# Seven block products in place of eight for the MLP's up projections of a fused two-layer trunk

## The chip, the cores and the metric

The kernel runs on one core of a Trainium2 chip. The metric is the device time of one execution in microseconds (us). Before the change it is 1857.52 us, the median of 3 runs (1856.43 to 1858.48).

## The reference, cut to what matters

The model is a decoder trunk of two layers over 528 positions (16 meta tokens and 512 tokens) with 1024 channels, all in float32. Each layer is

```
u = rms_norm(h, norm_mix);  proj = u @ w_in                  # 1024 -> 7168
conv branch, differential attention, sigmoid gates -> merged
h = h + merged @ w_o                                         # 1024 x 1024
u = rms_norm(h, norm_mlp)
h = h + square(relu(u @ w_up)) @ w_down                      # 1024 -> 4096 -> 1024
return h[:, 16:528]
```

The change is in the MLP, the last two of these lines. In the second layer the 16 meta positions are no longer needed there, so its MLP runs over 512 positions and that of the first over 528.

## The kernel before, in words

Channels lie on the 128 partitions, in 8 chunks, and positions on the free axis. Every weight is cut into slabs of 1024 rows by 256 columns (128 partitions x 2048 elements, 1 MB). A layer has 68 slabs in a fixed order: 8 of the GLU, 12 of v, q and k, 8 of gates, 4 of w_pw, 4 of w_o, and 32 of the MLP.

A product in float32 is made of three in the PE's rounded format, float32r: with w = w_hi + w_lo and u = u_hi + u_lo it is w_hi u_hi + w_hi u_lo + w_lo u_hi. So each slab passes these steps. SP's queue loads it into one of two buffers `w_raw[:, b]` (L493), after `w_ready` says that the slab two before it has been split. The high part is a rounding copy into `w_hi[:, b]` and the low part is `w_raw - w_hi` into `w_lo[:, b]`, in 16 pieces of 128 columns. In `split` (L503 to L516) POOL makes both, after a one-element `tick`; in `split_low` (L518 to L523) POOL makes the low part and ACT the high one (`w_high_part`, L955 to L960). Both need the buffer's former slab to be used up (`w_used`). The MLP's slabs all go through `split`, those of w_pw and w_o through `split_low`. PE takes a slab in `a_slabs`: for each of its two column halves `a_tile` (L614 to L626) runs over 8 row blocks, 3 parts, and 2 halves of the positions (264 columns) in the first layer or all of them at once (512 columns) in the second. This is 96 matmuls of 264 columns, or 48 of 512, for a slab. The two column halves go to two slots of two PSUM banks, and `a_free` says that a slot has been read.

The MLP's order is `MLP_ORDER`: up 0, up 1, down 0, up 2, down 1, up 3, down 2, down 3, each of 4 slabs. For an up tile, ACT takes relu out of PSUM (L1152) and squares it, rounded, as the high part of `hid` (L1154); DVE squares relu again (L1562) and subtracts (L1563). For a down tile, DVE multiplies PSUM by the norm's reciprocal (L1591) and adds it to `h` (L1592). `hid` has two buffers, the second one `hid_b`. Ahead of the MLP, in the slabs of w_o, DVE adds each of the 8 tiles to `h` (L1549); ACT scales it, rounded, as `u2`'s high part and squares it for the norm's sum (`norm_tile`); DVE makes the low part (L1538) and the sum (L1541).

Every engine works its own list in program order, so an instruction that waits holds all that stand behind it. `announce` and `link` make an engine wait for its own instruction to be finished before the next.

Of the kernel before, what the change touches and what calls it, by code (L numbers as in the profile page):

```python
# [244 lines left out]
def build(nc, x_t, w_slabs, pvecs, rows_in, ident_in, mask_in, identb_in, out, h_spill, r_rows):  # L245
    ctx = ExitStack()
    with ctx:
# [254 lines left out]
        def _(pool):  # L502
# [110 lines left out]
        def _(pe):  # L613
            def a_tile(layer, slot, b, col, src, full=False, waits=None, blocks=range(NT)):  # L614
# [36 lines left out]
            def a_slabs(layer, slab, tile, n_turns, src, ready, full=False, hooks=(), middle=None, begin=None):  # L651
# [3 lines left out]
                def body(i, hooks=()):  # L655
                    hooks = list(hooks)
                    for b in range(1 if begin and isinstance(i, int) else 0, 2):
                        pe.wait_ge(w_ready, i * 2 + (s0 + b + 1))
                        for col in range(2):
# [1001 lines left out]
```

## Time and profile before

| | |
|---|---|
| median of 3 runs | 1857.52 us (1856.43 to 1858.48) |
| the profiled execution's own time | 1856.81 us |
| its span, first to last instruction | 1855.0 us |
| PE busy (matmuls) | 1831.2 us, 99% |
| POOL busy | 1333.3 us, 72% |
| DVE busy | 1119.0 us, 60% |
| ACT busy | 577.0 us, 31% |
| mean granted TensorE clock | 0.999 |
| bytes moved by DMA | 160.66 MB, mean 87 GB/s |

The span of the profiled execution is 1.8 us under its own time; what lies around it is the start and the end of the program. The profiled execution is 0.7 us under the median. PE's busy time is the union of its matmuls, whose ends are modelled, so the start of each of them, not its length, tells the pace. The MLP of the first layer runs from about 578 to 956 us of the span, that of the second from about 1491 us to the end.

### The profile page before, as it was taken

The numbers are of one execution on the slowest core, as the hardware profiler recorded it, in microseconds if no ns is written. First come the engines' busy times: TensorE is split into PE (matmuls) and PEld (weight loads), VectorE is DVE, ScalarE is ACT, GpSimd is POOL, SyncE is SP. The second block draws the span as 40 slices with busy tenths as digits, with TensorE's granted clock in tenths as the row PEclk, the third lists the DMA queues.
The fourth block names the chain that finished last, engine by engine and source line by source line (L and its number), as shares of the span: only waits on it lengthen the run. The fifth ranks groups of instructions, "written<-read, shape, count | busy, mean of one in ns | idle before, by whom it ended". The sixth has DMA issues, their size and how long they took to land.

```text
span 1855.0 us, 34632 instructions
## 1 busy us (share of the span) xinstructions
PE 1831.2 (99%) x12787; PEld 1652.2 (89%) x12787; DVE 1119.0 (60%) x1666; ACT 577.0 (31%) x1616; POOL 1333.3 (72%) x2400
## 2 busy tenths in 40 slices
PE   9999999999999999999999999999999999999999
PEld 9999888898999999999999998887768877888887
DVE  7998887877544333333468989888885433333233
ACT  4135565536332110101011246664362322010100
POOL 3767454646778888888898663436477799898985
PEclk9999999999999999999999999999999999999999
DMA  4221021112322222222232211111124222222222
GB/s 178 91 92 66 28 69 47 47 69 85 135 96 79 86 93 90 91 91 106 109 120 91 91 69 47 69 47 48 67 91 146 105 91 91 91 91 91 90 107 74
DMA packets 25550, 160.66 MB, mean 87 GB/s; under 512 B 3024, under 2 KB 3408, under 8 KB 7776
## 3 DMA queue, kind: packets, MB, share of 16 engines
q1 hardware_dynamic: 21888, 147.01, 22.4%
q10 hardware_dynamic: 3552, 12.15, 1.7%
q8 instruction: 73, 1.20, 0.3%
q14 instruction: 37, 0.30, 0.1%
HBM read 154.85 MB, written 4.29 MB: 86 GB/s over the span
## 4 chain that ended last, share of the span: by engine, by line
PE 87%; POOL 7%; DVE 2%; issue 2%; ACT 2%; POOLq 0%; DVEq 0%; ACTq 0%
PE psum L625 63%; PE psum L714 15%; POOL w_lo L515 4%; PE psum L744 2%; PE psum L776 2%; PE psum L764 1%; POOL w_lo L522 1%; POOL w_hi L513 1%; ACT e L978 1%; PE psum L752 1%; DVE mx L1259 1%; PE psum L646 1%; PE psum L821 1%; PE psum L793 1%; PE psum L632 0%
## 5 line engine op out<-in xcount | busy, mean ns | idle before, releaser
L625 PE MATMUL psum<-u,w_hi 128*128 128x264 f32 (+1 forms) x4416 | 900.5, 316 | 9.7 <-POOL w_lo L515 5.6
L515 POOL TENSOR_TENSOR w_lo<-w_raw,w_hi 128x128 fp32r<-128x128 f32 x1504 | 759.9, 543 | 7.8
L625 PEld LDWEIGHTS psum<-u,w_hi 128*128 128x128 f32 x4416 | 666.8, 189 | 68.1 <-issue 9.1
L625 PE MATMUL psum<-u,w_lo 128*128 128x264 f32 (+1 forms) x2208 | 558.8, 313 | 0.0
L522 POOL TENSOR_TENSOR w_lo<-w_raw,w_hi 128x128 fp32r<-128x128 f32 x640 | 314.3, 530 | 123.1 <-ACT w_hi L960 83.8
L625 PEld LDWEIGHTS psum<-u,w_lo 128*128 128x128 f32 x2208 | 362.5, 189 | 25.0
L714 PE MATMUL psum<-w_hi,u 128*128 128x256 f32 (+1 forms) x1856 | 337.1, 284 | 2.6 <-ACT v_sb L936 1.5
L467 DVE SCALAR_TENSOR_TENSOR psum<-xg,pvec,psum 128x512 f32<-128x512 f32 x440 | 300.9, 751 | 4.6 <-DVE xg L1399 2.2
L714 PEld LDWEIGHTS psum<-w_hi,u 128*128 128x128 f32 (+1 forms) x1856 | 264.8, 172 | 11.5 <-issue 3.1
L714 PE MATMUL psum<-w_lo,u 128*128 128x256 f32 (+1 forms) x928 | 259.7, 280 | 0.0
L1562 DVE TENSOR_TENSOR relu<-relu 128x528 f32<-128x528 f32 (+1 forms) x64 | 66.2, 1034 | 234.8 <-ACT u L1154 119.7
L1152 ACT ACTIVATE relu<-psum 128x528 f32<-128x528 f32 (+1 forms) x64 | 38.7, 605 | 459.9 <-PE psum L625 459.9
L513 POOL TENSOR_SCALAR w_hi<-w_raw 128x2048 fp32r<-128x2048 f32 x94 | 180.4, 1919 | 0.0
L512 POOL TENSOR_TENSOR tick<-ones 128x1 f32<-128x1 f32 x94 | 19.8, 211 | 218.8 <-PE psum L625 196.4
L625 PE MATMUL psum<-hid_b,w_hi 128*128 128x264 f32 (+1 forms) x768 | 163.9, 322 | 0.1
L714 PEld LDWEIGHTS psum<-w_lo,u 128*128 128x128 f32 (+1 forms) x928 | 159.7, 172 | 3.7
L1591 DVE TENSOR_TENSOR down_tmp<-psum,r_inv 128x512 f32<-128x512 f32 (+1 forms) x56 | 39.1, 699 | 190.3 <-PE psum L625 190.3
L567 POOL TENSOR_TENSOR rtmp<-raw,tabs 128x640 f32<-128x640 f32 x16 | 25.0, 1562 | 153.1 <-DVE q_scale L1221 101.9
L625 PEld LDWEIGHTS psum<-hid_b,w_hi 128*128 128x128 f32 x768 | 118.7, 188 | 12.0 <-issue 0.6
L625 PE MATMUL psum<-hid_b,w_lo 128*128 128x264 f32 (+1 forms) x384 | 102.4, 321 | 0.0
L978 ACT ACTIVATE e<-psum,nb,q_scale 128x272 f32<-128x272 f32 (+4 forms) x144 | 83.8, 585 | 35.8 <-DVE nb L1265 35.8
L960 ACT CAST w_hi<-w_raw 128x2048 fp32r<-128x2048 f32 x40 | 76.6, 1915 | 48.6 <-PE psum L625 48.6
(190 smaller groups left out, 1963.0 us busy)
## 6 DMA issues: line engine op xcount, KB each, us to landing
w_raw<-w_slabs SPq DMA_DIRECT2D x135, 1024.0 KB, 4.9
h<-x_t SPq DMA_DIRECT2D x4, 528.0 KB, 7.2
h<-x_t ACTq DMA_DIRECT2D x1, 2112.0 KB, 10.7
h_spill<-h ACTq DMA_DIRECT2D x8, 264.0 KB, 2.2
h<-h_spill ACTq DMA_DIRECT2D x1, 2112.0 KB, 10.4
out<-h SPq DMA_DIRECT2D x8, 256.0 KB, 2.0
r_b<-r_rows ACTq DMA_DIRECT2D x1, 1584.0 KB, 6.5
r_b<-r_rows ACTq DMA_DIRECT2D x1, 1536.0 KB, 7.4
```

The lines of the kernel that those rows point to most:

```text
L467: return nc.vector.scalar_tensor_tensor(out=done if ends else acc, in0=x, scalar=w, in1=done if begins else acc, op0=ALU.mult, op1=ALU.add)
L513: chain.link(nc.gpsimd.tensor_scalar(w_hi[:, b, :], w_raw[:, b, :], 1.0, 1.0, ALU.mult, ALU.mult))
L515: last = nc.gpsimd.tensor_tensor(w_lo[:, b, c:c + P], w_raw[:, b, c:c + P], w_hi[:, b, c:c + P], ALU.subtract)
L522: last = nc.gpsimd.tensor_tensor(w_lo[:, b, c:c + P], w_raw[:, b, c:c + P], w_hi[:, b, c:c + P], ALU.subtract)
L625: last = nc.tensor.matmul(psum[:, 2 * slot + j, 0:n], w[:, b, cut], src[:, part, kc, at0:at0 + n], start=(kc == 0 and m == 0), stop=(kc == ...
L714: last = nc.tensor.matmul(psum[0:tn, n % 2, 0:2 * P], u[:, part, kc, t0:t0 + tn], w[:, b, kc * 2 * P:(kc + 1) * 2 * P], start=(kc == 0 and ...
L744: nc.tensor.matmul(psum[0:tn, banks[c], at0:at0 + k1 - k0], qk[rows64, 0, hh % 2, qp, t0:t0 + tn], qk[rows64, 1, hh % 2, kp, k0:k1], start ...
L960: nc.scalar.copy(w_hi[:, b, :], w_raw[:, b, :]).then_inc(w_high, 1)
L978: ins = nc.scalar.activation(e[0:tn, c, E_OFF[i]:E_OFF[i] + w], psum[0:tn, banks[c], S_AT[i]:S_AT[i] + w], ACT.Exp, bias=nb[0:tn, c, i:i + ...
L1152: nc.scalar.activation(row(relu[:, j, :], layer), a_ps(layer, j), ACT.Relu).then_inc(a_free[j], 1)
L1562: link(V.tensor_tensor(relu2[:, lo:lo + n], relu[:, j, lo:lo + n], relu[:, j, lo:lo + n], ALU.mult))
L1591: announce(dve, V.tensor_tensor(row(down_tmp[:], layer), a_ps(layer, j), row(r_inv2[:], layer), ALU.mult), a_free[j], a_read(layer, A_MLP ...
```

## The change: what it does

The up projections alone are computed by the scheme of Strassen in Winograd's form. A slab's 1024 rows and 256 columns are cut in two each way into quarters A11, A21, A12, A22 of 512 rows by 128 columns (the host lays them out so, `quads`), and the activations into quarters of 512 channels by half of the positions. From sums of weight quarters (S1 to S4) and of activation quarters (T1 to T4) seven products are made, where there were eight. Each is 4 row blocks x 3 parts = 12 matmuls of 264 columns (first layer) or 256 (second), 84 for a slab. They stand in the order p1, p5, p2, p6, p7, p4, p3, and `P_BANK` gives their PSUM banks; p1 and p6 share bank 6, p5 has bank 7, p7 bank 3.

The MLP's order becomes up 0, down 0, up 1, down 1, and so on. The down slabs take `split_low` on POOL and the high part from ACT (`down_high`). `hid` has one buffer. An up slab's four first forms (A11, S1, A12, S2) get their low part in another way: ACT writes the rounded negative into `w_lo` (`early_neg`), and two DMAs that POOL issues add `w_raw` and `s2` to it in place (`early_low`). The three other forms (A22, S3, S4) keep POOL's subtraction, 4 pieces of 128 columns each (`late_parts`). DVE makes the sums of weights and of products. The diff is condensed below: several statements stand on one line, and waits are named after `#`.

```
+A_TILES = A_MLP + 32
+MLP_ORDER = [(what, g) for g in range(4) for what in ("up", "down")]
+PRODUCTS = [(F_A11, G_B11, "p1"), (F_S1, G_T1, "p5"), (F_A12, G_B21, "p2"), (F_S2, G_T2, "p6"), (F_S3, G_T3, "p7"), (F_A22, G_T4, "p4"), (F_S4, G_B22, "p3")]
+P_BANK = {"p1": (6, 6), "p6": (6, 6), "p5": (7, 7), "p2": (0, 4), "p3": (1, 5), "p4": (2, 2), "p7": (3, 3)}
 SP, the load of the slab two ahead of up slab m:
+    sp.wait_ge(low_landed[n % 2], 32 * (n // 2 + 1)); sp.wait_ge(w_form, n + 1); sp.wait_ge(late_low, 2 * n + 1); sp.wait_ge(sum_late, n + 1)
 POOL:
+def early_low(g, m):
+    pool.wait_ge(w_neg, n + 1)
+    chain.link(nc.gpsimd.tensor_tensor(tick[:], ones[:, 0:1], ones[:, 0:1], ALU.mult))
+    pool.dma_start(w_lo[:, b, 0:3 * QUAD], w_raw[:, b, 0:3 * QUAD], accum_op=ALU.add).then_inc(low_landed[b], 16)
+    pool.dma_start(w_lo[:, b, 3 * QUAD:SLAB], s2[:, b, :], accum_op=ALU.add).then_inc(low_landed[b], 16)
+def late_parts(g, m, parts):      # per part: wait w_late, 4 x tensor_tensor 128x128 into x_lo
+order: early_low(g,1) | late_parts(g,1,plain) early_low(g,2) late_parts(g,1,summed) late_parts(g,2,plain) early_low(g,3)
+       late_parts(g,2,summed) late_parts(g,3,all) | 4 x down_low | early_low(g+1,0) late_parts(g+1,0,all)
 PE:
+def up_products(layer, g, m):
+    pe.wait_ge(low_landed[b], ...); pe.wait_ge(w_form, n + 1); pe.wait_ge(c22_done, n)
+    # p6: p1_done; p2: a_free of both slots (m < 2) or hid_ready 2(n-1); p7: hid_ready 2n-1, late_low 2n+2; p3: w_ready s+1
+    for kc in range(KH):
+        for j, (w, act_) in enumerate([(hi, uh), (hi, ul), (low, uh)]):
+            last = nc.tensor.matmul(quad(layer, m, name), w[:, cut], act_[:, x, kc, 0:n2], ...)
 ACT, in the slabs of w_o, tile i:
+    if i == NT - 3: early_neg(layer, 0, 0)
+    if i == NT - 1: early_neg(layer, 0, 1)
+    norm_raw(layer, i); form_plain(layer, i)
+    if i == NT - 1: late_plain(layer, 0, 0)
+    form_sum(layer, i)
+    if i == NT - 1: first_product(layer, 0, 0); late_sums(layer, 0, 0)
+    if i >= KH: form_last(layer, i)
+    norm_square(layer, i)
+    if i == NT - 2: early_high(layer, 0, 0)
+    if i == NT - 1: early_high(layer, 0, 1)
 ACT, up slab m:
+    if m == 3: down_high(layer, g, 0)
+    if m == 0 and g: early_neg(layer, g, 1)
+    if m or g: first_product(layer, g, m)
+    if m == 1 and g == 0: late_sums(layer, g, 1)
+    if m: hidden_high(layer, g, m - 1, 0)              # relu, then its square
+    if m == 1 and g == 0: early_neg(layer, g, 2)
+    if m < 3: late_plain(layer, g, m + 1)
+    if m < 3 and (m or g): early_high(layer, g, m + 1)
+    if m == 1 or m == 0 and g: early_neg(layer, g, m + 2)
+    if m < 3 and (m or g): late_sums(layer, g, m + 1)
+    hidden_high(layer, g, m, 1)
+def early_neg: wait sum_early; wait w_used s-1 (m < 2) or q_full of p6 two slabs before; 2 x nc.scalar.mul(..., -1.0), 1536 and 512 columns
+def early_high: 2 x nc.scalar.copy, 1536 and 512 columns;  late_plain: copy of 512;  late_sums: wait sum_late; copy of 1024
 DVE, in the slabs of w_o, tile ch: add to h;  if ch == 7: sums_late(0, 0);  form_norm(ch);  if ch in (4, 5): sums_early(0, ch - 4)
 DVE, up slab m:
+    if m: c12_sum(g, m - 1); (g, m) == (0, 1): read the norm's sum; hidden_low(g, m - 1, 1); square_up(g, m - 1, 0)
+    if m == 1 and g == 0: sums_early(g, 2)
+    if m < 3 and (m or g): sums_late(g, m + 1)
+    if m: hidden_low(g, m - 1, 0)
+    if m == 1 or m == 0 and g: sums_early(g, m + 2)
+    u2_sum(g, m); c22_sum(g, m); c21_sum(g, m); square_up(g, m, 1)
+    if m == 0 and g == 0: sums_late(g, 1)
+def sums_early: 2 dependent tensor_tensor of 512 columns in w_raw and s2;  sums_late: wait w_ready of the slab before; 2 of 512
+def u2_sum: wait p6; U2 = p6 + P1, T = p5 + U2;  c22_sum: p2 += P1; wait p7; U3 = p7 + U2; p7 = p5 + U3 -> c22_done
+def c21_sum: wait p4; p4 += U3 -> tile_sum;  c12_sum: wait p3; p3 += T -> tile_sum
+def square_up: wait relu; in place in PSUM max(x, 0) * relu;  hidden_low: wait its square; subtract -> hid_ready
+form_norm(ch), ch < 4: wait u_raw; T1; 2 subtractions; the sum of squares.  ch >= 4: T2, T4, T3 (264), 3 subtractions (528, 264, 528), the sum
 DVE, down slab d of g < 3: if d == 3: sums_late(g + 1, 0);  after its first tile, d > 1: sums_early(g + 1, d - 2)
```

## Rows read from the trace of the kernel before

**Rows 1.** The page, part 1 (PE's line) and part 2 (the granted clock by slice).
```profile
PE 1831.2 (99%) x12787; PEld 1652.2 (89%) x12787; DVE 1119.0 (60%) x1666; ACT 577.0 (31%) x1616; POOL 1333.3 (72%) x2400
...
PEclk9999999999999999999999999999999999999999
```
**Rows 2.** The page, part 4: the chain that ended last, by engine and line.
```profile
PE 87%; POOL 7%; DVE 2%; issue 2%; ACT 2%; POOLq 0%; DVEq 0%; ACTq 0%
PE psum L625 63%; PE psum L714 15%; POOL w_lo L515 4%; PE psum L744 2%; PE psum L776 2%; PE psum L764 1%; POOL w_lo L522 1%; POOL w_hi L513 1%; ACT e L978 1%; PE psum L752 1%; DVE mx L1259 1%; PE psum L646 1%; PE psum L821 1%; PE psum L793 1%; PE psum L632 0%
```
**Rows 3.** Windows: stretch, length, busy of PE, PEld, DVE, ACT, POOL; clock, DMA.
```profile
588.00:681.50 93.50, 93.36 (x764) 93.02 (x763) 32.71 (x34) 18.88 (x30) 84.24 (x145) 1.00 0.26 90
1491.50:1580.40 88.90, 88.28 (x378) 70.38 (x377) 34.77 (x37) 19.82 (x32) 84.09 (x140) 1.00 0.27 95
```
**Rows 4.** Timeline of PE, first layer, up slab: start, length, instruction, count.
```profile
870.47 0.65 PE L625 MATMUL psum<-u,w_hi 128*128 128x264 f32 x4
...
879.23 0.65 PE L625 MATMUL psum<-u,w_hi 128*128 128x264 f32 x4
```
**Rows 5.** Timeline of PE, second layer.
```profile
1599.96 0.62 PE L625 MATMUL psum<-u,w_hi 128*128 128x512 f32 x2
...
1603.43 0.64 PE L625 MATMUL psum<-u,w_hi 128*128 128x512 f32 x2
```
**Rows 6.** Timeline of PE, products of 256 columns for q, k and v.
```profile
249.92 0.40 PE L714 MATMUL psum<-w_hi,u 128*128 128x256 f32 x2
...
253.46 0.40 PE L714 MATMUL psum<-w_hi,u 128*128 128x256 f32 x2
```
**Rows 7.** Groups by line and form, ACT: count, busy us, mean ns, idle before.
```profile
L960 ACT CAST w_hi<-w_raw 128x2048 fp32r<-128x2048 f32 x40 | 76.6, 1915 | 48.6 <-PE psum L625 48.6
L945 ACT COPY raw<-psum 128x256 f32<-128x256 f32 x64 | 23.6, 368 | 47.0 <-PE psum L714 46.7
L1152 ACT ACTIVATE relu<-psum 128x528 f32<-128x528 f32 x32 | 19.6, 612 | 235.5 <-PE psum L625 235.5
L1154 ACT ACTIVATE hid_b<-relu 128x528 f32 x16 | 10.4, 648 | 2.1
```
**Rows 8.** The same groups on DVE.
```profile
L1592 DVE TENSOR_TENSOR h<-h,down_tmp 128x528 f32 x24 | 32.6, 1360 | 3.8 <-DVE down_tmp L1591 3.8
L1562 DVE TENSOR_TENSOR relu<-relu 128x528 f32<-128x528 f32 x32 | 34.3, 1072 | 120.4 <-ACT u L1154 61.4 <-ACT hid_b L1154 59.0
L1591 DVE TENSOR_TENSOR down_tmp<-psum,r_inv 128x512 f32<-128x512 f32 x32 | 22.1, 692 | 106.4 <-PE psum L625 106.4
L1591 DVE TENSOR_TENSOR down_tmp<-psum,r_inv 128x528 f32<-128x528 f32 x24 | 17.0, 708 | 83.9 <-PE psum L625 83.9
L467 DVE SCALAR_TENSOR_TENSOR psum<-xg,pvec,psum 128x512 f32<-128x512 f32 x440 | 300.9, 751 | 4.6 <-DVE xg L1399 2.2 <-DVE o_ms L1293 0.2
```
**Rows 9.** Timeline of DVE: an instruction that waits for the one before it.
```profile
634.54 0.71 DVE L1563 TENSOR_TENSOR hid_b<-relu,hid_b 128x528 f32 x1 [0.18 <-DVE relu L1562]
```
**Rows 10.** Timeline of POOL: an MLP slab's split, and a low part alone (w_o).
```profile
545.04 7.89 POOL L522 TENSOR_TENSOR w_lo<-w_raw,w_hi 128x128 fp32r<-128x128 f32 x16 [4.45 <-ACT w_hi L960]
...
613.61 0.19 POOL L512 TENSOR_TENSOR tick<-ones 128x1 f32<-128x1 f32 x1 [1.00 <-PE psum L625]
613.76 1.91 POOL L513 TENSOR_SCALAR w_hi<-w_raw 128x2048 fp32r<-128x2048 f32 x1
615.76 8.49 POOL L515 TENSOR_TENSOR w_lo<-w_raw,w_hi 128x128 fp32r<-128x128 f32 x16
```
**Rows 11.** Timeline of DVE: the last tiles of w_o are added to h.
```profile
560.64 0.71 DVE L1549 TENSOR_TENSOR h<-psum,h 128x528 f32<-128x528 f32 x1 [3.59 <-PE psum L625]
...
578.16 0.71 DVE L1549 TENSOR_TENSOR h<-psum,h 128x528 f32<-128x528 f32 x1 [3.44 <-PE psum L625]
```
**Rows 12.** The page, parts 3 and 6: the slabs' queue and one load.
```profile
q1 hardware_dynamic: 21888, 147.01, 22.4%
...
w_raw<-w_slabs SPq DMA_DIRECT2D x135, 1024.0 KB, 4.9
```

More of the change, by code:

```diff
@@ new lines, in late_parts @@
+                def late_parts(g, m, parts):
+                    b, n = m % 2, up_nth(layer, g, m)
+                    for k in parts:
+                        source = w_raw[:, b, 3 * QUAD:SLAB] if k == 0 else s34[:, (k - 1) * QUAD:k * QUAD]
+                        if k < 2:
+                            pool.wait_ge(w_late, 2 * n + k + 1)
+                        for c in range(0, QUAD, P):
+                            cut = slice(k * QUAD + c, k * QUAD + c + P)
+                            last = nc.gpsimd.tensor_tensor(x_lo[:, b, cut], source[:, c:c + P], x_hi[:, b, cut], ALU.subtract)
+                        last.then_inc(late_low if k < 2 else w_ready, 1)
@@ L649, in first_slab, with a_slabs @@
                             last.then_inc(w_used if col else a_full, 1)
-            def a_slabs(layer, slab, tile, n_turns, src, ready, full=False, hooks=(), middle=None, begin=None):
+            def a_slabs(layer, slab, tile, n_turns, src, ready, full=False, hooks=(), middle=None, begin=None, pairs=False):
                 s0, n0 = layer * SLABS + slab, layer * A_TILES + tile
@@ L669, in body @@
                             else:
-                                last = a_tile(layer, 2 if third else col, b, col, src, full, ready if not (b or col) else None)
+                                last = a_tile(layer, 2 if third else col, b, col, src, full, ready if not (b or col) else None, pairs=pairs)
                             last.then_inc(w_used if col else a_full, 1)
@@ L682, in partition_sums, with mlp_sums @@
+            def mlp_sums(layer):
+                source, sums = mlp_sum(layer)
+                pe.wait_ge(n_summed, layer + 1)
+                for j in range(2):
+                    last = nc.tensor.matmul(sums[:, j, :], ones[:], source[:, j, :], start=True, stop=True)
+                last.then_inc(st_full, 1)
             def partition_sums(layer, ready, value, src, full=False, cols=False):
@@ L1168, in _ @@
                             act.dma_start(h_spill[:, ch, :], h[:, ch, :]).then_inc(spilled, 16)
+                    else:
+                        down_high(layer, g, 2)
+                        down_high(layer, g, 3)
+                        if g < 3:
+                            early_neg(layer, g + 1, 0)
+                            late_plain(layer, g + 1, 0)
+                            late_sums(layer, g + 1, 0)
+                            early_high(layer, g + 1, 0)
         @block.vector
@@ L1596, in down_body @@
                                     link(ins)
-                        turns(dve, NT // 2, down_body, chain, 0 if g == 3 else 2)
+                                if j == 0 and d > 1 and g < 3:
+                                    sums_early(g + 1, d - 2)
 def kernel(**inputs):
```

441 lines of the change are left out of this document (370 added, 71 removed).

## The prediction

> **What bounds the kernel now.** Read the page's busy shares first, then the chain, then the windows of the MLP. PE is busy 99% of the span at a granted clock of nine tenths or more in every slice, the upper of its two levels, 2.4 GHz [rows 1]. The chain that ended last is 87% PE, and 63% is the one matmul line L625; POOL follows with 7%, nearly all of it splits [rows 2]. In the windows of two up stages (eight slabs) PE has no gap worth naming: 93.36 of 93.50 us, 88.28 of 88.90 us [rows 3]. So a matmul less is time won, as long as no other engine becomes late. In the same windows POOL is busy 84 us, 90% and 95%, while DVE has 33 to 35 us and ACT 19 to 20: one engine has almost no room and two have much [rows 3].
>
> **What is removed.** The pace is read from starts. First layer: from 870.47 to 879.23 are 12 periods of 6 matmuls, 0.1217 us each for 264 columns [rows 4]. Second: 15 matmuls of 512 columns in 3.47 us, 0.231 each [rows 5]. 256 columns with a weight load each, as the new products have, stand at 30 matmuls in 3.54 us, 0.118 each [rows 6]; so the extra weight loads of the second layer are in that pace already. An up slab goes from 96 x 0.1217 = 11.68 to 84 x 0.1217 = 10.22 us, and from 48 x 0.231 = 11.1 to 84 x 0.118 = 9.9. With 16 up slabs a layer that is 23.4 + 19.1 = **42.5 us** at most. It is kept only where everything else fits into 10.2 or 9.9 us a slab.
>
> **Prices.** ACT: 2048 columns 1.915, 528 take 0.648, so 0.834 ns a column: 1536 and 512 together 2.12, 1024 1.06, 512 0.63; relu 0.61; the copy of a product 0.37 [rows 7]. DVE: 692 and 708 ns for 512 and 528 columns give 1 ns a column, 264 columns 0.44; relu's square in place as L467, 0.77 [rows 8]; each instruction that waits for its forerunner adds 0.18 [rows 9]. POOL: 0.49 a piece (7.89 / 16) [rows 10]. Where both DVE operands lie in SBUF and POOL is at work, 264 to 528 columns wait: L1562 takes 1.07 against 0.71 for the same form right behind it, L1592 1.36 [rows 8, 9]. I take 0.36 more where POOL works, and 0 where it waits; the ends are 0 and 0.65. A pair `sums_early` is then 1.74, `sums_late` 1.38, plus that.
>
> **The new DMAs.** No row shows a DMA that adds, or one issued by POOL. One from HBM to SBUF of the same 1 MB lands after 4.9 us [rows 12]; the slabs' queue has 22.4% of 1855 us for 147 MB, 2.96 us for 1 MB, so 1.9 us of the 4.9 are fixed. The lower end is 4.9. With two issues at 0.3 each (between POOL's tick of 0.19 and something above it [rows 10]) it is 5.5, which I take, as the nearest row moves the same bytes. If the bytes pass three times, 3 x 2.96 + 1.9 + 0.6 = 11.4 is the upper end. The Trainium skill speaks against my value: Collectives: The Full Stack, section The bandwidth ceiling, says that an adding transfer reads two sources and so runs at half the rate of a copy. By rows its data part would be 5.9 and the landing 8.4 us; that is the first rival. The page DMA: Bandwidth & Descriptors, section Latency and other measured facts, has about 1 us to the first byte for a DMA from GpSimd against 0.6 from SP; that would make my 5.5 about 5.9, and the sum 0.8 us longer.
>
> **The start of each MLP.** Let T be the end of w_o's matmuls (578.1), with tiles 4 to 7 full at T-17.5, -11.7, -5.8, 0 [rows 11]. For a tile above 3, DVE adds (0.71), waits for ACT's scaling (0.71 with hops), makes T2, T4, T3 (0.44 each, two waits), three subtractions (0.71, 0.44, 0.71) and the sum (0.89): 5.85, all of a tile's 5.84. `sums_early` comes on top at tiles 4 and 5. So tile 4 is left at T-9.6. Then ACT makes `early_neg` (2.12) ahead of its scaling of tile 5, and DVE leaves tile 5 at T-0.7. ACT's square of tile 6 ends at T+3.3 and `early_high(0, 0)`, behind it, at T+5.5: the first product starts there, not at T. On ACT follow `early_neg` 7.6, scaling of tile 7 8.3, plain forms 8.9 and 9.5, T2's form 9.95, the product's copy 10.3, `late_sums` 11.4; POOL's four pieces of S3 end at 13.4. p7 waits for these, and p7, p4 and p3 take 4.4 us: slab 0 ends at T+17.8 instead of 10.2 or 9.9. **Loss 7.6 + 7.9 = 15.5 us.** Ends: 11 (no ACT delay, no port waits) and 19 (port waits at 0.65).
>
> **Slab 1 of the first group** starts at T+17.8. DVE: square_up 18.9, sums_late 20.3, c12 20.9, the norm's sum 21.7, hidden_low 22.4; ACT's late_sums and relu end at 21.9, square_up 23.4, sums_early(2) with a port wait 25.4. ACT's early_neg(2) ends at 27.5, the DMAs land at 33.0. DVE's own list (sums_late after POOL's parts 27.9, hidden_low, sums_early, five sums of products) brings `c22_done` at 33.1, the same. Slab 2 should have started at 28.4. **Loss 4.7 + 5.0 = 9.7**; it grows by 2 us for each us that the landing grows.
>
> **Slab 1 of the six later groups.** From its start: p1 full 1.65, copy 2.05, relu 2.65, square_up 3.65, slab 1's low parts ready 3.7, sums_late 5.3, hidden_low 6.0, sums_early 7.7, then U2, T, P2 + P1, U3, p7's sum (3 x 0.62 + 2 x 0.44) 10.45. The next p1 waits for it: 0.2 over 10.22, 0.55 over 9.9. **Loss 2.3.** Its own start needs the landing of `early_neg(1)`, which can't begin before the down slab is used up: negative ready at +2.4, due at 10.2 or 9.9, so 7.8 or 7.5 us are there, and at 5.5 nothing is lost.
>
> **From up to down.** The first down slab takes the buffer of up slab 2. After that one is used up: ACT 1.92, POOL 16 x 0.49 = 7.9, hops, 10.0 us against slab 3's 10.22 or 9.9. But `down_high` stands behind relu and square of slab 2's tile, whose chain (c21_sum 20.6 after slab 1's start + 10.4 + 10.2) ends 1.3 or 1.6 late: loss 0.9 and 1.55, in the two first groups 0.2 and 0.5, where slab 2 started late. 3 x 0.9 + 3 x 1.55 + 0.7 = **8.1**. Before, POOL had 1.0 us of idle time here [rows 10]: the room is spent.
>
> **Down slabs.** POOL's 7.9 and ACT's 1.9 stand in 11.68 or 11.1 us; DVE's sums for the next group hold POOL twice. 1.5 us in all, ends 0 and 5. SP's loads come 5 us or more ahead of their use in every place above. The move of the order, relu2's loss and `hid` in one buffer cost nothing: down's row blocks 6 and 7 are needed 4.4 us after its start and are ready 1.1 us before; if that cover goes, it costs the same us.
>
> **Sum.** 15.5 + 9.7 + 2.3 + 8.1 + 1.5 = 37.1 lost of 42.5, 5.4 gained. The profiled execution took 1856.8 (span 1855.0 and 1.8 around it): 1851.4, and with 0.7 to the median **1852 us**.
>
> **Rivals.** (1) Slower: the bytes of the adding DMAs pass twice or more, since source and destination are both read, and they land late. At 8.4 us: 2 x 2.9 more at the first groups, 3 x 0.6 + 3 x 0.9 more at slab 1 of the others, 10.3: 1862. At 11.4 it is 2 x 5.9, 3 x 3.6 + 3 x 3.9, and slab 0, which has 9.3 us, loses 2.1 in six groups: 47, 1899. It turns slower than before by more than 3.7 us at about 8.4. For it: no row shows such a DMA at the copy's pace; against it: the engines are 22% used [rows 12]. (2) The chain on DVE is the bound: port waits of 0.65, as L1592 shows [rows 8], on each pair in slab 1 and at the starts give 6 x 0.6 + 3 = 6.6 more, 1858, no change. Against it: POOL waits much of the time. (3) The starts are cheaper, 11 and 6, and the turns to down cost nothing where ACT slips in earlier: 42.5 - 25 = 17 gained, 1841. For it: each of my chains takes the latest of several arrivals. That the products don't save their matmuls is excluded by rows 4 to 6.
>
> **Chances.** Forecast 38%, within 1846 to 1858; rival 1 30%; rival 2 17%; rival 3 15%. A measurement tells 0.2% (3.7 us) from no change. Faster: all of rival 3 and 27 of the forecast's 38, 42%; same 22%; slower 36%. The range, 1838 to 1885, takes in rival 3 and most of rival 1.
>
> **What would show it.** Right: an up slab's PE stretch of 10.2 and 9.9 us in slabs 2 and 3; the first product 5 us or more after w_o's last matmul, released by ACT w_hi; slab 2 of a first group released by the DMA; idle PE of 1 to 2 us ahead of each down stage, released by POOL w_lo. Wrong: a landing of the adding DMAs over 8 us, PE gaps ahead of slab 1 in later groups, or DVE busy under 8 us in a slab. A time under 1841 or over 1885 would say that a term is missing.

## The result and the profile after

The changed kernel takes 1882.51 us (1880.9 to 1883.81, 4 runs) where the kernel before takes 1856.97 on the same chip (1855.56 to 1858.48, 4 runs): ratio 1.0134, 95% interval 1.0122 to 1.0146. It is 25.5 us slower; 5 us faster was forecast. All readings below are of the profiled execution, span 1881.4 us, 26.4 longer than that of before.

The page first: PE's line, the granted clock by slice, and part 4 of the changed kernel.
```profile
PE 1809.6 (96%) x13173; PEld 1660.0 (88%) x13173; DVE 1296.5 (69%) x2074; ACT 832.9 (44%) x1912; POOL 1160.3 (62%) x2240
...
PEclk9999999999999999999999999999999989999999
...
PE 73%; POOL 7%; DVE 6%; DMA 6%; issue 4%; ACT 3%; DVEq 0%; POOLq 0%; ACTq 0%
PE psum L757 41%; PE psum L896 15%; PE psum L849 9%; DMA w_raw<-w_slabs 3%; DMA w_lo<-s 3%; POOL w_lo L597 3%; PE psum L926 2%; PE psum L958 2%; POOL w_lo L604 2%; PE psum L946 1%; POOL x_lo L715 1%; ACT e L1252 1%; PE psum L934 1%; DVE h L1991 1%; PE psum L778 1%
```
PE's share of the chain fell from 87% [rows 2] to 73%, and two transfers stand in it that were not there: the slab loads and the DMAs that add, 3% each. In busy time PE saved 21.6 us (1831.2 less 1809.6), but the span shows the waits. The same windows as in [rows 3], same columns (PE, PEld, DVE, ACT, POOL, granted clock, DMA share, GB/s). They hold other slabs now: the second begins in the last tiles of w_o, whose matmuls end at 1501.0 us here.
```profile
588.00:681.50 93.50, 85.82 (x687) 85.14 (x686) 53.24 (x78) 38.27 (x47) 62.60 (x132) 0.96 0.48 131
...
1491.50:1580.40 88.90, 77.95 (x475) 70.79 (x474) 55.36 (x91) 45.56 (x62) 52.25 (x108) 0.92 0.49 129
```
PE has 7.7 and 11.0 us of gaps (4.7 of the 11.0 are the wait for the first product of the second MLP) where it had almost none, and the clock is below the 1.00 of before.

**Where the time went.** An undisturbed up slab takes 10.19 us (84 matmuls, 0.1214 each) in the first layer and 9.97 (0.1187) in the second. Sixteen slabs each save 16 x 1.49 + 16 x 1.13 = 41.9 us (42.5 forecast). With the 26.4 us that the span grew, 68.3 us were lost again. Slab by slab, from PE's starts, in us (what a slab takes above 10.19 or 9.97, its wait at the end among it):

| place | forecast | measured |
|---|---|---|
| start of each MLP, to the start of slab 1 | 7.6 + 7.9 | 8.4 + 9.0 |
| first groups, slab 1 | 4.7 + 5.0 | 6.6 + 5.9 |
| first groups, slab 2 | 0 | 1.6 + 2.8 |
| six later groups, slab 0 | 0 | 6.4 |
| six later groups, slab 1 | 2.3 | 17.7 |
| six later groups, slab 2 | 0 | 9.2 |
| slab 3 and the turn to down | 8.1 | 0.8 |
| down slabs | 1.5 | about 3 |
| sum | 37.1 | 71.4 |

(The sum is 3.1 above 68.3: it charges every wait against an even pace, and the kernel before isn't at that pace throughout either. Its first MLP, 578.2 to 953.4 us, takes 1.4 us more than 32 x 11.68. In the other direction, 1.2 us of the 26.4 lie between the two MLPs, and part of them may be a stretch of 3.4 us at half clock at 1398 us, which the kernel before doesn't have there.) Of the 34 us that the forecast lacks, 31 stand in one kind of place, slabs 0 to 2 of the later groups: 33.3 us for 2.3.

**One such wait.** Group 1, first layer; slab 1 runs from 692.93. Timelines of POOL, SP's queue, DVE, ACT and PE (start, length, instruction, and in brackets the idle time before it and what ended it):
```profile
690.57 0.19 POOL L702 TENSOR_TENSOR tick<-ones 128x1 f32<-128x1 f32 x1 [1.26 <-ACT w_lo L1158]
691.06 0.89 POOL L703 DMA_DIRECT2D w_lo<-w_raw  x1 [0.30 <-POOL tick L702]
691.64 1.20 POOL L704 DMA_DIRECT2D w_lo<-s  x1
...
692.90 9.53 SPq L574 DMA_DIRECT2D w_raw<-w_slabs  x2
...
697.88 0.70 DVE L1928 TENSOR_TENSOR hid<-psum,hid 128x528 fp32r<-128x528 f32 x1
702.75 0.69 DVE L1850 TENSOR_TENSOR w_raw<-w_raw 128x512 f32<-128x512 f32 x1 [4.17 <-DMA w_raw<-w_slabs]
703.48 0.69 DVE L1851 TENSOR_TENSOR s<-w_raw 128x512 f32<-128x512 f32 x1
704.21 0.43 DVE L1898 TENSOR_TENSOR r_inv<-psum,r_inv 128x264 f32<-128x264 f32 x1
...
705.82 0.44 DVE L1907 TENSOR_TENSOR psum<-psum,q_u 128x264 f32<-128x264 f32 x1
...
704.21 1.48 ACT L1157 ACTIVATE w_lo<-w_raw 128x1536 fp32r<-128x1536 f32 x1 [5.51 <-DVE s L1851]
...
706.41 0.56 PE L849 MATMUL psum<-uh,w_hi 128*128 128x264 f32 x1 [2.99 <-DVE psum L1907]
```
SP's row holds two issues, the second at 702.10, so its length is not a landing. The load of slab 3 can't be issued before slab 1's low parts have landed, since the adding DMA reads `w_raw` too: 692.90. At that moment slab 2's adding DMAs are 1 to 2 us old. They share the 16 engines, and the load lands at 702.73, after 9.8 us for the usual 4.9. DVE has stood since 698.6 at the sums of slab 3, with the sums of C22 queued behind; PE, ready at 703.4, starts slab 2 at 706.4. All six later groups go this way: the load is issued at the start of slab 1 and takes 7.7 to 10.4 us, and DVE stands idle for 2.1 to 4.3 us. With the usual 4.9 us it would have landed at 697.8 (an estimate from these rows), before DVE asks for it. So it is the meeting of the two queues, on top of the late issue, that makes it late. The DMA view of 688 to 706 us shows the sharing (packets, MB, share of 16 engines; then KB and us to landing):
```profile
q0 software_dynamic: 544, 1.90, 59.9%
q1 hardware_dynamic: 262, 2.02, 30.3%
...
w_raw<-w_slabs SPq DMA_DIRECT2D x2, 1024.0 KB, 7.5
w_lo<-w_raw POOLq DMA_DIRECT2D x1, 768.0 KB, 6.6
w_lo<-s POOLq DMA_DIRECT2D x1, 256.0 KB, 10.4
```
The same bytes hold the engines twice as long when they are added: 18 x 0.599 / 1.90 = 5.7 us for 1 MB against 2.7. Over the whole execution, the page:
```profile
q1 hardware_dynamic: 21888, 147.01, 22.7%
q0 software_dynamic: 9216, 33.56, 9.7%
...
w_raw<-w_slabs SPq DMA_DIRECT2D x135, 1024.0 KB, 4.9
w_lo<-w_raw POOLq DMA_DIRECT2D x32, 768.0 KB, 6.0
w_lo<-s POOLq DMA_DIRECT2D x32, 256.0 KB, 7.0
```
0.097 x 1881.4 / 33.56 = 5.44 us per MB against 2.90 for the slabs. The Trainium skill, Collectives: The Full Stack, section The bandwidth ceiling, says of the reduce transfers of a ring that each add needs two source reads and so halves the rate of a copy. The trace agrees (1.9 times), though these transfers stay inside one SBUF.

**The clock.** Windows of the changed kernel, columns as above; the last is undisturbed work:
```profile
582.40:586.00 3.60, 3.51 (x17) 3.54 (x18) 2.30 (x5) 3.57 (x5) 1.32 (x3) 0.54 0.02 5
609.70:616.60 6.90, 3.07 (x14) 3.07 (x15) 2.65 (x5) 2.40 (x5) 5.29 (x11) 0.52 1.02 194
705.20:712.30 7.10, 5.89 (x27) 5.92 (x28) 4.35 (x9) 5.94 (x10) 5.71 (x13) 0.53 0.75 178
716.00:719.00 3.00, 3.00 (x27) 3.00 (x26) 1.80 (x5) 0.33 (x1) 3.00 (x8) 1.00 0.78 320
```
After PE's waits at 578, 607 and 703.4 us the granted clock is 0.5, the lower level (1.2 GHz), and the first matmuls of the next slab start 0.21 to 0.22 us apart for 0.12. There are eight such stretches with some 155 matmuls: about 14.8 us, counted in the table's first, third and sixth lines. Some 4 us of them cost nothing: the 42 slow matmuls in slab 0 of the two first groups stand ahead of p7, which waits for POOL afterwards all the same (1.5 us in the first layer, 0.7 in the second). The prediction had no such term.

### The profile page after: what moved, and what is told of

Read it like the earlier page. It is cut to its first block, busy times and chain, and to the rows that moved or that the text cites. A ratio compares the mean times of both kernels' runs of the same rounds, so it can differ in the third digit from the quotient of the medians.

```text
span 1881.4 us, 35177 instructions
## 1 busy us (share of the span) xinstructions
PE 1809.6 (96%) x13173; PEld 1660.0 (88%) x13173; DVE 1296.5 (69%) x2074; ACT 832.9 (44%) x1912; POOL 1160.3 (62%) x2240
## 3 DMA queue, kind: packets, MB, share of 16 engines
q0 software_dynamic: 9216, 33.56, 9.7%
## 4 chain that ended last, share of the span: by engine, by line
PE 73%; POOL 7%; DVE 6%; DMA 6%; issue 4%; ACT 3%; DVEq 0%; POOLq 0%; ACTq 0%
PE psum L757 41%; PE psum L896 15%; PE psum L849 9%; DMA w_raw<-w_slabs 3%; DMA w_lo<-s 3%; POOL w_lo L597 3%; PE psum L926 2%; PE psum L958 2%; POOL w_lo L604 2%; PE psum L946 1%; POOL x_lo L715 1%; ACT e L1252 1%; PE psum L934 1%; DVE h L1991 1%; PE psum L778 1%
## 5 line engine op out<-in xcount | busy, mean ns | idle before, releaser
L604 POOL TENSOR_TENSOR w_lo<-w_raw,w_hi 128x128 fp32r<-128x128 f32 x1152 | 548.9, 515 | 234.5 <-ACT w_hi L1234 195.2
L757 PE MATMUL psum<-u,w_hi 128*128 128x264 f32 (+1 forms) x2112 | 408.0, 308 | 8.9 <-POOL w_lo L597 5.0
L757 PEld LDWEIGHTS psum<-u,w_hi 128*128 128x128 f32 x2112 | 310.1, 189 | 31.1 <-POOL w_lo L597 6.5
L757 PE MATMUL psum<-hid,w_hi 128*128 128x264 f32 (+1 forms) x1536 | 328.4, 322 | 1.8 <-POOL w_lo L604 1.6
L757 PEld LDWEIGHTS psum<-hid,w_hi 128*128 128x128 f32 x1536 | 237.1, 188 | 26.6 <-issue 2.3
L757 PE MATMUL psum<-u,w_lo 128*128 128x264 f32 (+1 forms) x1056 | 251.1, 304 | 0.0
L597 POOL TENSOR_TENSOR w_lo<-w_raw,w_hi 128x128 fp32r<-128x128 f32 x480 | 237.4, 532 | 2.5
L757 PE MATMUL psum<-hid,w_lo 128*128 128x264 f32 (+1 forms) x768 | 204.8, 321 | 0.0
L849 PE MATMUL psum<-uh,w_hi 128*128 128x264 f32 (+1 forms) x512 | 154.2, 301 | 43.1 <-DVE psum L1907 17.2
L757 PEld LDWEIGHTS psum<-u,w_lo 128*128 128x128 f32 x1056 | 170.6, 189 | 8.5
L849 PE MATMUL psum<-ul,w_hi 128*128 128x264 f32 (+1 forms) x512 | 151.7, 296 | 0.0
```

Of the source, the lines that this page charges most:

```text
L597: last = nc.gpsimd.tensor_tensor(w_lo[:, b, c:c + P], w_raw[:, b, c:c + P], w_hi[:, b, c:c + P], ALU.subtract)
L604: last = nc.gpsimd.tensor_tensor(w_lo[:, b, c:c + P], w_raw[:, b, c:c + P], w_hi[:, b, c:c + P], ALU.subtract)
L757: last = nc.tensor.matmul(psum[:, 2 * slot + j, 0:n], w[:, b, cut], src[:, part, kc, at0:at0 + n], start=(kc == 0 and m == 0), stop=(kc == ...
L849: last = nc.tensor.matmul(quad(layer, m, name), w[:, cut], act_[:, x, kc, 0:n2], start=(kc == 0 and j == 0), stop=(kc == KH - 1 and j == 2))
```

## The experiments

Each run was timed in three rounds beside the kernel before, whose median on each chip was 1857.0 to 1857.7. Ratios are to it. "After" is the changed kernel, timed apart from these runs; the last column is the difference of the medians.

| run | us | ratio | 95% interval | us against after |
|---|---|---|---|---|
| e1_copy | 1841.08 | 0.9912 | 0.9896 to 0.9929 | -41 |
| e2_behind | 1896.04 | 1.0211 | 1.0194 to 1.0228 | +14 |
| e3_warm | 1877.22 | 1.0102 | 1.0086 to 1.0119 | -5 |
| e4_order | 1858.54 | 1.0003 | 0.9993 to 1.0012 | |
| e5_start | 1890.3 | 1.0182 | 1.0165 to 1.0199 | +8 |
| e6_half | 1846.41 | 0.9946 | 0.9929 to 0.9962 | -36 |
| e7_both | 1858.36 | 1.0009 | 0.9999 to 1.0020 | -24 |
| e8_behind_high | 1888.92 | 1.0172 | 1.0155 to 1.0189 | +6 |
| e9_split | 1841.65 | 0.9920 | 0.9903 to 0.9936 | -41 |
| e10_best | 1841.46 | 0.9917 | 0.9900 to 0.9934 | -41 |
| e11_first | 1876.18 | 1.0099 | 1.0082 to 1.0116 | -6 |
| e12_after_c21 | 1842.49 | 0.9925 | 0.9898 to 0.9953 | -40 |

**Copies for additions (e1_copy).**
```diff
-  pool.dma_start(w_lo[...], w_raw[...], accum_op=ALU.add)
+  pool.dma_start(w_lo[...], w_raw[...])        # and the same for s2
```


> The changed kernel with its 64 adding DMAs made plain copies of the same bytes (the low parts of the four early forms are then wrong). Theory A, the adding DMAs hold the 16 engines twice as long as a copy and push back the load of slab 3, whose sum blocks DVE's list: the software queue's share falls from 9.7% to about 5%, the landing from 7 to about 5 us, the load of slab 3 from 8 to 10 us back to 5, the PE gap ahead of slab 2 in the six later groups from 2.9 us each to under 1, and the first groups' gap by 2 to 3 us each; in all 15 to 22 us less, clock included, 1860 to 1867 us. Theory B, DVE's own chain with waits for the port it shares with POOL sets the gap: 0 to 4 us less, the gaps stay.

The copy leaves out the addition, so the four low parts hold the raw weights and sums. Every wait and byte count stays. 41 us went with the addition, where 15 to 22 were expected. Its queue and landings (the page), and group 1 of the first layer as windows, first of this kernel, then of the changed one:
```profile
q0 software_dynamic: 9216, 33.56, 5.1%
...
w_lo<-w_raw POOLq DMA_DIRECT2D x32, 768.0 KB, 4.0
w_lo<-s POOLq DMA_DIRECT2D x32, 256.0 KB, 4.6
```
```profile
669.20:704.50 35.30, 35.30 (x293) 35.30 (x293) 26.46 (x40) 23.09 (x31) 22.03 (x48) 1.00 0.61 201
```
```profile
669.20:704.50 35.30, 34.04 (x278) 33.62 (x277) 21.26 (x30) 18.59 (x24) 19.47 (x38) 1.00 0.78 188
```
0.051 x 1839.1 / 33.56 = 2.8 us per MB: a copy from SBUF to SBUF has the slabs' pace. The two windows are the same stretch of time, not the same work: group 1 begins at 676.0 us here and at 682.4 in the changed kernel. All 24 slabs of the later groups then take 10.19 or 9.97 us without a gap, and the turn to down costs nothing although slab 2 is on time. So what the adding DMAs cost in the later groups is the addition and not that there are DMAs at all. Most of it lies in the transfer: the landing of the first falls by 2.0 us, of which POOL's issue has 0.3 (0.57 us for 0.89).

**Sums of slab m+2 behind the sums of C22 (e2_behind).**
```diff
-  if m == 1 or m == 0 and g: sums_early(g, m + 2)
   u2_sum(g, m)
   c22_sum(g, m)
+  if m == 1 or m == 0 and g: sums_early(g, m + 2)
```


> The changed kernel with DVE's sums_early of slab m+2 behind c22_sum of slab m, where it stood ahead of u2_sum. Theory A (DVE's list is held by a late load, and c22_done behind it holds PE): the gap ahead of slab 2 in the later groups falls from 2.9 us to under 1, the stall partly coming back as a wait of p7 for POOL's late parts of slab 2; 5 to 12 us less in all. Theory B (the length of the chain of sums, not the wait for the load): sums_early's 1.5 us leave the chain, so at most 1.5 us each in six groups, and the gap ahead of slab 2 in the first groups, which waits for the landing, stays.

If DVE's order were the cause, the gap ahead of slab 2 would go. It went from 17.7 to 12.4 us in the six later groups, and a new one of 2.5 us came ahead of slab 3 in each; both theories expected a faster kernel, and it is 14 us slower. Slab 2's own adding DMAs now go out 0.5 to 2.1 us after the start of slab 1, for 1.4 to 3.1 us ahead of it, and land at 10.3 to 12.1. PE's first matmuls of slabs 2 and 3, group 1:
```profile
704.60 0.36 PE L849 MATMUL psum<-uh,w_hi 128*128 128x264 f32 x1 [1.99 <-DVE psum L1907]
...
719.05 0.36 PE L849 MATMUL psum<-uh,w_hi 128*128 128x264 f32 x1 [2.29 <-DVE psum L1907]
```
The sums, the negative and the adding DMA of slab 3 are one loop with the loads; what is put back in one place comes due in the next.

**Dummy matmuls in PE's waits (e3_warm).**
```diff
+  if (g, m) == (0, 0): 18 matmuls of ones into an unused bank
+  if m == 2: 24 of them (8 in later groups), ahead of the wait for slab 2
   pe.wait_ge(low_landed[b], 32 * (n // 2 + 1))
```


> The changed kernel with matmuls of ones by ones in PE's waits: 18 ahead of the first up slab of a layer, 24 ahead of slab 2 of the first group, 8 ahead of slab 2 of the later groups. Theory C, PE's idle time there is followed by a stretch at the lower granted clock that costs 14.8 us beside the gaps themselves: the granted clock stays at 1.0 through the MLP, and 8 to 14 us less. Rival: the slow stretches come from something else (the DMA traffic, POOL), and the clock falls all the same: no change, or slower by what the added matmuls overrun.

The clock's mean rose from 0.988 to 0.996, and of eight slow stretches in the MLPs two were left, one in slab 0 of each layer. Only 5.3 us were won: in group 1, slab 1's start to slab 3's start is 23.5 us for 26.4, but slab 0 of the first group took 15.1 for 13.6 us, with a wait of 2.5 us at p7. There p7 starts 13.4 us after w_o's last matmul in both kernels, since POOL's low parts set it; the faster first products only made the wait ahead of it longer, and the half clock came behind it (18 matmuls, 17 in the second layer). The same place as above, 705 us, in windows of this kernel and of the changed one:
```profile
700.00:723.00 23.00, 22.22 (x182) 21.88 (x182) 15.26 (x27) 13.56 (x18) 13.54 (x30) 1.00 0.57 162
```
```profile
703.00:719.30 16.30, 13.31 (x88) 13.13 (x87) 11.91 (x21) 9.70 (x13) 10.36 (x23) 0.79 0.72 195
```
So the clock's share is real, but it is won back only where no later wait of the same slab takes it. In one of the six later groups the dummies also ran past the wait, and slab 2 started 0.65 us later, counted from slab 1's start, than without them.

**The order alone (e4_order).** The kernel before, with up and down groups alternating.
```diff
-MLP_ORDER = [("up", 0), ("up", 1), ("down", 0), ("up", 2), ...]
+MLP_ORDER = [(what, g) for g in range(4) for what in ("up", "down")]
```


> The kernel before with the MLP's order alone changed to up 0, down 0, up 1, down 1. All theories: within 1 us of the kernel before, since the hidden chunks 6 and 7 are ready 1 us or more ahead of use. A rival: each of the 8 turns from up to down waits 0.5 us or more, 4 us slower.

No change: this part of the edit is free, as forecast.

**Half of the adding DMAs' bytes (e6_half).**
```diff
-  scalar.mul(w_lo[0:3Q], w_raw[0:3Q], -1.0); scalar.mul(w_lo[3Q:4Q], s2, -1.0)
+  scalar.mul(w_lo[0:2Q], w_raw[0:2Q], -1.0)
-  pool.dma_start(w_lo[0:3Q], w_raw[0:3Q], accum_op=add); pool.dma_start(w_lo[3Q:4Q], s2, accum_op=add)
+  pool.dma_start(w_lo[0:2Q], w_raw[0:2Q], accum_op=add)
+  # VectorE, after w_form: w_lo[2Q:3Q] = w_raw[2Q:3Q] - w_hi[2Q:3Q]; w_lo[3Q:4Q] = s2 - w_hi[3Q:4Q]
```


> The changed kernel with half of the adding DMAs' bytes: ScalarE's negatives and the adding DMA cover the block A11 and the sum S1 alone (512 KB in one DMA for 1 MB in two), and the low parts of A12 and S2 are made by VectorE as raw minus high, two 512-column subtractions a slab, placed where VectorE is idle. Theory A (the loop slab load, sums, negative, adding DMA, next load is what binds the later groups, and the second pass of the adding DMA's bytes is what makes it too long): landing falls from 6-7 us to 3.5-4.5 us, the gaps ahead of slab 2 in later groups (1.2 to 4.0 us) go, granted clock is full there, total 1840 to 1850, near the 1841 that plain copies gave. Rival (a fixed cost of an adding DMA, its issue and latency, not its bytes): landing stays over 5.5 us and the total at 1870 to 1880. Second rival (VectorE, 8.7 of 10.2 us busy in slab 1, now gets 1.4 us more): PE waits for the sums of C22 or for the hidden tiles in slabs 1 and 2, 1855 to 1875.

The edit has one more part, which the cut leaves out: in the last down slab ACT copies the high parts of the next slab 0 ahead of its late parts. What that part is worth alone was not run; e7, e9, e10 and e12 have it too.

1846.4: 36 us below after, 11 below before. The landing is 4.6 us. The gaps ahead of slabs 1 and 2 are gone in the later groups and the clock there is full. There the load of slab 3 goes out 2.9 to 3.5 us ahead of slab 1's start, where it went out at that start before, and lands 2.4 to 3.7 us into it. The first product of each MLP also comes 0.9 us earlier, which fits the shorter negatives ahead of its high copy on ACT. One wait is new, at p2 of slab 2, 1.1 to 1.3 us in the six later groups. DVE, POOL and PE around it:
```profile
695.84 0.44 DVE L1921 TENSOR_TENSOR psum<-psum,q_u 128x264 f32<-128x264 f32 x1
696.32 3.89 DVE L1859 TENSOR_TENSOR w_lo<-w_raw,w_hi 128x512 fp32r<-128x512 f32 x1
700.13 0.68 DVE L1860 TENSOR_TENSOR w_lo<-s,w_hi 128x512 fp32r<-128x512 f32 x1
...
696.00 3.65 POOL L716 TENSOR_TENSOR x_lo<-s,x_hi 128x128 fp32r<-128x128 f32 x8
...
700.86 0.39 PE L852 MATMUL psum<-uh,w_hi 128*128 128x264 f32 x1 [0.93 <-DVE w_lo L1860]
```
Two equal subtractions took 3.89 and 0.68 us. The first begins 0.3 us behind the start of eight POOL subtractions in a row and ends 0.6 us after them.

**Away from POOL's run (e9_split).** Its low part of A12 for slab 2 moved ahead of `u2_sum` of slab 1, where POOL stands; the one of S2 stays.
```diff
+  if m == 1: low_form(g, 2, A12)
   u2_sum(g, m); c22_sum(g, m); c21_sum(g, m)
-  if m in (1, 2): low_form(g, m + 1, A12 and S2)
+  if m in (1, 2): low_form(g, m + 1, S2 if m == 1 else A12 and S2)
```


> The kernel with half of the adding DMAs' bytes, and VectorE's low part of A12 for slab 2 moved from behind the C21 sum to ahead of the U2 sum of slab 1 (the low part of S2 stays behind). In its parent that 512-column subtraction took 3.9 us for its usual 0.69 because it began beside a back-to-back run of eight GpSimd subtractions, and PE's p2 of slab 2 waited 1.2 to 1.4 us in all eight groups. Theory (the place beside the GpSimd run is what costs): the wait at p2 goes, total 1846.4 less 8 x 1.3 = 1836, 1834 to 1840. Rival (VectorE's slack of 1 us in slab 1 is used up, so the sums of C22 come late by as much): 1842 to 1848.

The wait at p2 of slab 2 is gone in every group, and 4.8 us of the hoped 10 came, a time between the theory's and the rival's: waits of 0.35 us came ahead of slab 3 in the second layer and of 0.36 to 0.56 at the end of slab 3 in both, and the first groups, to the end of slab 3, stayed within 0.4 us. POOL's run still holds DVE, now at the subtraction that stayed (slab 1 of group 1, second layer):
```profile
1597.50 3.33 DVE L1863 TENSOR_TENSOR w_lo<-s,w_hi 128x512 fp32r<-128x512 f32 x1
```
It took 3.1 to 3.3 us in all eight groups. Moving it away from POOL's run as well was not tried.

**The first group as the others (e10_best, e11_first).** Sums, negative and adding DMA of slab 2 go out during slab 0; e10 on top of e9, e11 on top of after.
```diff
   c21_sum(g, m)
+  if m == 0 and g == 0: sums_early(g, 2)          # DVE; was ahead of sums_late at m == 1
+  if m == 1 and g == 0: early_neg(layer, g, 2)    # ACT; was behind hidden_high
   first_product(layer, g, m)
-  late_parts(g, 1, plain + summed); early_low(g, 2)
+  late_parts(g, 1, plain); early_low(g, 2); late_parts(g, 1, summed)   # POOL
```


> As the kernel before it in this list, and the first group treated as the later ones: sums, negative and adding DMA of slab 2 are issued during slab 0 and the turn to slab 1, ahead of the first product's copy and the summed low parts of slab 1. Theory (the 3.4 us gap ahead of slab 2 of the first group and the slow clock after it come from where slab 2's early chain stands in the written order): gap under 1 us, no half clock in slab 2, 4 to 5 us less in each layer, 1826 to 1832. Rival (the wait moves to p7 of slab 1, whose low parts are made later, or to the gap ahead of slab 1): 1834 to 1840.

> The changed kernel with that treatment of the first group alone (the adding DMAs carry all their 1 MB). If the gap of 6.5 and 5.8 us ahead of slab 2 in the first group is made by the written order, it falls to the 2 to 4 us of the later groups, with less half-clock time: 1882.5 less 2 x (3 to 5) = 1872 to 1877. If it is made by the adding DMA's landing, 1879 to 1884.

e10: 1841.46, no change from e9, where its theory had 1826 to 1832 and its rival 1834 to 1840. e11: 6.3 us below after, as its first theory said; the gap ahead of slab 2 fell there from 6.5 and 5.8 to 4.0 and 4.1. What is left of it in e10 has another releaser, the load of slab 3:
```profile
604.25 0.69 DVE L1854 TENSOR_TENSOR w_raw<-w_raw 128x512 f32<-128x512 f32 x1 [0.35 <-DMA w_raw<-w_slabs]
...
608.50 0.43 PE L854 MATMUL psum<-uh,w_hi 128*128 128x264 f32 x1 [2.92 <-DVE psum L1920]
```

**Slab 3's sums behind C21, first group only (e12_after_c21).**
```diff
-  if m == 1 or m == 0 and g: sums_early(g, m + 2)     # ahead of u2_sum
+  if g and m < 2: sums_early(g, m + 2)
   u2_sum; c22_sum; c21_sum
+  if m == 1 and g == 0: sums_early(g, 3)
```


> The best kernel so far (half of the adding DMAs' bytes, the split low part, the first group's slab 2 early) with VectorE's sums of slab 3 in the first group alone moved behind the C21 sum of slab 1. There the load of slab 3 lands 9.7 us into slab 1, and the sums of C22 stood behind it in VectorE's order. Theory (in the first group, unlike in the later ones, it is the order on VectorE that makes the gap ahead of slab 2): the gap of 3.2 and 3.0 us falls under 0.5 us, slab 2 runs at full clock, nothing new ahead of slab 3, 1841.5 less 6 to 9 = 1832 to 1836. Rival (the loop through the adding DMA binds here too, as it did in the later groups when the sums were moved behind): the gap comes back ahead of slab 3, 1839 to 1843.

The rival held. PE's first matmul of slab 2, its p6, and the first of slab 3:
```profile
606.64 0.36 PE L854 MATMUL psum<-uh,w_hi 128*128 128x264 f32 x1 [1.10 <-DVE psum L1920]
...
612.05 0.36 PE L854 MATMUL psum<-uh,w_hi 128*128 128x264 f32 x1 [0.79 <-ACT r_inv L1189]
...
619.87 0.36 PE L854 MATMUL psum<-uh,w_hi 128*128 128x264 f32 x1 [1.75 <-DVE psum L1920]
```
One gap of 3.2 us became three (start to start 1.4, 1.1, 2.0 with the matmul's own 0.12 in each), and slab 3 starts at 619.9 where it started at 620.3.

**The start (e5_start, e7_both).**
```diff
   norm_raw(layer, i)
-  if i == NT - 1: early_neg(layer, 0, 1)                # stood ahead of norm_raw
+  if i == NT - 2: early_high(layer, 0, 0)               # now ahead of norm_raw
   norm_square(layer, i)
+  if i == NT - 1: early_neg(layer, 0, 1); early_high(layer, 0, 1)
```


> The changed kernel with ScalarE's order at the start of an MLP alone changed: the high parts of up slab 0 are copied two output tiles earlier (ahead of the raw norm copy of channel 6), and the negatives of slab 1 stand behind the last channel's forms, just ahead of slab 1's high parts. Theory (what holds the first product is the 2.0 us high copy queued behind the forms of channel 6, and what holds the first slab's p2 and p7 is the last channel's forms queued behind slab 1's negatives): first product at T+2.0 to T+3.0 instead of T+4.45 and T+5.08, slab 0 ends 2 us earlier in each layer, total 1877 to 1880. If slab 1's adding DMAs, now issued some 6 us later, become the bound at once: slab 1 starts no earlier and the time is 1881 to 1887. Rival (the start is set by VectorE's forms of the last channel): first product earlier, but p2 waits longer by the same amount, 1881 to 1884.

> The two edits above together (half of the adding DMAs' bytes; high parts of slab 0 earlier at the start of an MLP). Theory A: the gains add up, since the later groups' loop and the start are different places: 1836 to 1846. Rival: with the loop relaxed the start gains nothing more, time as with half of the bytes alone.

Both missed: 1890.3 for e5 where no theory went above 1887, and 1858.4 for e7 where 1836 to 1846 was expected. In e5 the first product came at once, 0.5 us after the last w_o matmul for 4.45, and slab 0 took 22.3 us for 13.6:
```profile
578.65 0.39 PE L849 MATMUL psum<-uh,w_hi 128*128 128x264 f32 x1 [0.24 <-DMA w_lo<-s]
...
594.63 0.59 PE L849 MATMUL psum<-uh,x_hi 128*128 128x264 f32 x1 [5.22 <-POOL x_lo L715]
```
POOL issues slab 1's adding DMAs ahead of slab 0's late low parts; with the negatives moved back, it waits for them and p7 waits for POOL. My theory had moved an instruction on ACT and not asked who stands behind its reader on POOL.

**The first product's copy behind the high parts (e8_behind_high).**
```diff
-  first_product(layer, g, m)
   hidden_high(layer, g, m - 1, 0); late_plain(...); early_high(layer, g, m + 1)
+  first_product(layer, g, m)
```


> The changed kernel with one part of the edit undone: ScalarE's copy of the first product stands behind the high parts of the coming slab (still ahead of the negatives of the slab after it). Theory: PE's p6 waits for that copy, which then ends 5.3 to 6.0 us into a slab for 4.4 us needed, so each of 24 to 32 up slabs loses 0.9 to 1.6 us: 1905 to 1925. Rival (PE waits later in the slab for the adding DMAs' loop anyway, so that the earlier wait is free where the gap ahead of slab 2 shrinks by as much): 1882 to 1895.

6 us slower than after: the rival's answer. p6 waits 0.75 to 2.3 us in most slabs, slab 1's among them (in the two first groups it waits 6 us there, and the gap ahead of slab 2 is gone):
```profile
698.95 0.39 PE L849 MATMUL psum<-uh,w_hi 128*128 128x264 f32 x1 [0.72 <-ACT r_inv L1185]
```
but the gap at the slab's end falls by a part of it (2.96 us for 3.27 in group 1). So this part of the edit is worth 6 us as the kernel stands; what it is worth where the loop doesn't bind was not run.

## Why the prediction was wrong

- **The pace.** Right: 10.19 and 9.97 us for 10.22 and 9.9, 41.9 us for 42.5.
- **The start.** Right in size (17.4 us for 15.5) and in mechanism: the first product is released by the high copy that stands behind the forms of tile 6, at T+4.4 (5.5 forecast), and p7 by POOL at T+13.4 in the first layer, as worked out. Of the difference 0.7 us in each layer is the norm's sum, four matmuls that PE runs between slabs 0 and 1 and that the sum didn't count.
- **Slab 1 of the first groups.** Right in mechanism, 12.4 us for 9.7: slab 2 is released by the adding DMA, whose landing took 7.9 us in the first layer for the 5.5 of the sum.
- **Slabs 0 to 2 of the later groups: the step that failed.** It was the sentence that SP's loads come 5 us or more ahead of their use in every place. The load of slab 3 is issued when slab 1's low parts have landed and is wanted some 6 us into slab 1; it landed 7.7 to 10.4 us in. I followed each landing to PE, and not to the next load that waits for it, and I counted each transfer as if it were alone. The places cost 33.3 us for 2.3; 6.4 of these are slab 0's wait for slab 1's landing, which I had put at nothing. e1, e2 and e6 show it from three sides: the addition taken away (33 us of these places gone), DVE's order changed (the gap only moves), half of the bytes (the gaps at the slabs' ends gone). Two of the prediction's signs of being wrong are there as well: gaps ahead of slab 1 in all six later groups (0.3 to 1.8 us), and landings over 8 us.
- **The DMAs that add.** The landing was mis-sized: from the first issue to the last landing 7.1 to 8.0 us alone and over 11 beside a load (691.06 to 702.09), for 5.5. Rival 1 named the cause and had the sign, but with 1862 at a landing of 8.4 us it was 20 us short, as it shared the missing step and counted no meeting of the two queues.
- **From up to down: 8.1 forecast, 0.8 found.** e1 has slab 2 on time and no wait at the turn either, so a late slab 2 is not what covers it; the chain of latest arrivals on ACT was too pessimistic, as rival 3 said.
- **The clock.** 14.8 us by count, some 4 of them hidden ahead of p7, missing from the sum. It is not a separate cause: each stretch follows a wait. e3 gave back 5.3 of it.
- **DVE's port waits** (what the prediction calls the extra time of a DVE instruction while POOL works) were charged at 0.36 a pair. Mostly they are 0 to 0.3, but a few in the up slabs of the changed kernel are 1.0 to 1.9 us and some in its down slabs up to 3.1, and in e6 there are some of 3.2, where an instruction begins beside a long POOL run. Rival 2, which had them as the bound, is out: in e1 DVE is busy for 8.70 us of slab 1's 10.20 in group 1, in the changed kernel for 7.93 of 13.48, and it is e1 in which PE doesn't wait.
- **The range and rival 3.** 1882.5 lies inside 1838 to 1885, but by luck: the upper part was there for a landing of up to 11.4 us, and at the landing found alone, 7.1 to 8.0, the prediction's own sums stay below 1862. The direction was wrong. Rival 3 was added up wrong as well: its 11 and 6 with the 2.3 and 1.5 of the forecast's sum are 20.8 and not 25, so its time was 1836 and not 1841, below the range that was to take it in.

What stays open: the start and the first group. e1's span of 1839.1 us is 26 above what the pace alone would give (1855.0 less 41.9), nearly all of it there. e12 suggests that there, too, it is the loop and not one order; what its shortest form is was not found. How much of the later groups' loss is the halved rate of the addition and how much its meeting with the load was not separated: e1 and e6 change both. e9 and e10 are the best versions, 15 us below the kernel before and 41 below the change.

## What to carry to other kernels

When a buffer's release hangs on a new transfer, walk the whole loop (release, load, what is made of it, transfer, release) and compare its length with the time between two uses, with the transfers' overlap counted; the landing of one transfer taken alone says little. Price an adding DMA by the bytes that it reads and writes, and give it only the part that no idle engine can take. And where PE gets a wait of over 2 us, look at the granted clock behind it: here eight of nine such waits were followed by matmuls at half pace, which cost time unless a later wait in the same slab took it up.

## What the runs showed of the hardware

- An SBUF to SBUF DMA that adds took 5.44 us of the 16 engines per MB, the same bytes as a copy 2.8 (e1). Beside a slab load both stretched: 10.4 us and 9.8 us to landing for 7.0 and 4.9.
- Issuing one from GpSimd takes 0.89 us on POOL's stream, a second right behind it 1.20 (they overlap, 0.58 apart); plain copies take 0.57 and 0.53.
- A 512-column subtraction on DVE with both operands in SBUF took 0.69 us, but 3.9 when it began beside eight POOL subtractions in a row, and 6.7 beside sixteen (in e7). In the first group of e12 a subtraction of the same form (608.46 us) took 0.69, with POOL idle.
- The clock's fall is not sure after a wait. In the changed kernel's MLPs PE waited nine times for 2.4 to 6.5 us at one stroke; after eight of them the granted clock was 0.5 (1.2 GHz) for 3.4 or 6.8 us, and after one of 3.65 us (at 1625 us) it stayed at 1. After none of the shorter waits there (up to 1.9 us) did it fall.
